# Half of a normalised input multiplied between modulation slabs, thirteen places for late slabs, and the last recurrent gates moved behind a gate tile

## The reference: one decoder layer, cut to what matters

```python
mod = silu(c) @ w_ada + b_ada            # (9, 6144): six blocks of 1024
sh1, sc1, g1, sh2, sc2, g2 = split(mod, 6)
h = rmsnorm(x, norm_pre_mix) * (1 + sc1) + sh1
q, k, v, g, xr, gr = split(h @ w_in)     # xr, gr: 1536 wide, 12 tiles of 128
...                                      # retention over q, k, v, gated by g
xc = causal_conv(xr)                     # 4 taps
r = sigmoid(xc @ w_rg_a + b_rg_a); i = sigmoid(xc @ w_rg_x + b_rg_x)   # block diagonal, 12 blocks
a = exp(-8 * r * softplus(-lru_param))
hseq = scan(a, sqrt(1 - a * a) * i * xc) # the recurrence over time
rnn_y = hseq * gelu(gr)
ga, gb = sigmoid(h @ w_mgate + b_mgate)  # 8 tiles each
mixed = (ga * (ret_y @ w_br_ret) + gb * (rnn_y @ w_br_rnn)) @ w_out
x = x + g1 * rmsnorm(mixed, norm_post_mix)
h2 = rmsnorm(x, norm_pre_ffn) * (1 + sc2) + sh2
x = x + g2 * rmsnorm((silu(fg) * fu) @ w_ffn_out, norm_post_ffn)       # fg, fu = split(h2 @ w_ffn_in)
```

## Time and profile before

| | |
|---|---|
| median of three runs | 1472.25 us (1471.32 to 1474.86) |
| the profiled execution's own time | 1477.67 us |
| its span | 1475.9 us |
| granted clock of PE, mean over the span | 0.974 |
| PE busy | 95% of the span |
| DVE, ACT, POOL busy | 51%, 35%, 12% |
| data moved | 172.71 MB, mean 117 GB/s |

### The profile page before, as it was taken

How to read it: one execution, slowest core, us unless ns; L and a number is a source line. 1 busy time by engine, 2 the same in 40 slices (tenths; PEclk the granted TensorE clock), 3 DMA queues, 4 the chain that set the end, 5 groups by cost and what they waited for, 6 DMA issues and landing times.

```text
span 1475.9 us, 24107 instructions
## 1 busy us (share of the span) xinstructions
PE 1397.5 (95%) x10324; PEld 1301.5 (88%) x10324; DVE 759.6 (51%) x1042; ACT 515.5 (35%) x715; POOL 183.1 (12%) x284
## 2 busy tenths in 40 slices
PE   5799999899999999999999999999889999999995
PEld 2799998777897798799879888999789999999995
DVE  3459888412245476348536753875843333332225
ACT  4376778111233331333234233335422222222221
POOL 1022231000013213302220330000000000000000
PEclk8799999999899899999999999999999999999998
DMA  8312222466524325423441443235012222222331
GB/s 334 114 58 86 72 73 71 143 228 241 189 72 157 122 94 176 156 84 115 162 152 65 157 158 115 83 102 206 1 57 86 87 87 86 87 85 78 90 92 61
DMA packets 49931, 172.71 MB, mean 117 GB/s; under 512 B 5536, under 2 KB 7712, under 8 KB 49568
## 3 DMA queue, kind: packets, MB, share of 16 engines
q1 hardware_dynamic: 39456, 135.51, 27.6%
q0 software_dynamic: 9216, 33.56, 6.6%
q10 hardware_dynamic: 1152, 2.10, 0.4%
HBM read 149.82 MB, written 21.32 MB: 116 GB/s over the span
## 4 chain that ended last, share of the span: by engine, by line
PE 64%; DVE 6%; issue 1%; DMA 1%; ACT 1%; SPq 0%; DVEq 0%
PE ps L746 51%; PE ps L755 3%; PE ps L969 2%; PE ps L980 2%; PE ps L952 1%; PE ps L996 1%; PE ps L1006 1%; PE ps L998 1%; DMA raw<-in_w_out 1%; DVE x_res L1851 1%; DVE rsn L1846 1%; DVE mo L1850 1%; DVE s_lo L1667 1%; PE ps L909 0%; PE ps L922 0%
## 5 line engine op out<-in xcount | busy, mean ns | idle before, releaser
L746 PE MATMUL ps<-h_hi,w_hi 128*128 128x272 f32 x2096 | 445.4, 294 | 17.5 <-DVE w_lo L1484 10.3
L746 PE MATMUL ps<-h_hi,w_lo 128*128 128x272 f32 x2096 | 438.1, 291 | 0.0
L746 PE MATMUL ps<-h_lo,w_hi 128*128 128x272 f32 x2096 | 436.8, 290 | 0.0
L1484 DVE TENSOR_TENSOR w_lo<-raw,w_hi 128x1024 fp32r<-128x1024 f32 (+2 forms) x190 | 228.7, 1206 | 335.6 <-ACT w_hi L1146 332.5
L746 PEld LDWEIGHTS ps<-h_hi,w_hi 128*128 128x128 f32 x2096 | 336.2, 191 | 23.7 <-issue 8.9
L746 PEld LDWEIGHTS ps<-h_lo,w_hi 128*128 128x128 f32 x2096 | 334.1, 191 | 0.0
L746 PEld LDWEIGHTS ps<-h_hi,w_lo 128*128 128x128 f32 x2096 | 331.8, 191 | 0.0
L1146 ACT ACTIVATE w_hi<-raw 128x1024 fp32r<-128x1024 f32 (+2 forms) x190 | 195.4, 1029 | 306.3 <-PE ps L746 161.6
L1767 DVE SCALAR_TENSOR_TENSOR state<-state,ps 128x512 f32<-128x512 f32 x64 | 41.1, 683 | 113.5 <-PE ps L1006 113.4
L746 PE MATMUL ps<-a_hi,w_hi 128*128 128x272 f32 x308 | 64.4, 291 | 2.1 <-DVE a_lo L1493 2.1
L746 PE MATMUL ps<-a_lo,w_hi 128*128 128x272 f32 x308 | 64.4, 290 | 0.0
(11 more groups left out here) (242 smaller groups left out, 1953.0 us busy)
## 6 DMA issues: line engine op xcount, KB each, us to landing
raw<-in_w_head SPq DMA_DIRECT2D x48, 512.0 KB, 3.6
raw<-in_w_fin SPq DMA_DIRECT2D x38, 512.0 KB, 3.5
ada_late<-in_w_ada SPq DMA_DIRECT2D x32, 512.0 KB, 4.3
state<-in_state POOLq DMA_DIRECT2D x32, 512.0 KB, 4.1
out_rs<-state POOLq DMA_DIRECT2D x32, 512.0 KB, 3.4
raw<-in_w_rnn SPq DMA_DIRECT2D x24, 512.0 KB, 3.6
ada_raw<-in_w_ada SPq DMA_DIRECT2D x16, 512.0 KB, 14.8
raw<-in_w_bret SPq DMA_DIRECT2D x16, 512.0 KB, 3.5
```

Of the source, the lines that this page charges most:

```text
L746: mm = nc.tensor.matmul(dst[:, half, :], a, b[:, half * HALF:(half + 1) * HALF], start=first and j == 0, stop=last and j == 2)
L1484: V.tensor_tensor(lo[:, 0:cols], raw_slab(i)[0][:, 0:cols], hi[:, 0:cols].bitcast(F32), ALU.subtract).then_inc(lo_ready, 1)
```

## The change

Four edits.

1. **Start.** PE turns the row of block 0 right after block 0. Block 1 accumulates in bank 7 (after ACT has read the sums of squares there), and between its slabs PE multiplies the first half of `h`: after slabs 1 to 4 one k-step of `xr` 0 each, after slabs 5 and 6 two k-steps of `gr` 0 each. Then it turns the row of block 1, and multiplies the second half of `h` into both tiles. DVE makes `w_lo` of `xr` 0 before `first_input(0)`; ACT does the first splits only in the first of its two rounds.
2. **Late slabs.** `ADA_RING` is 13: three places as before, ten in the memory of the recurrences (`rec`), which may be filled once all of `y` and the outputs of the recurrences are made. The first three are loaded behind `rg_w`.
3. **SP's loop** issues, for part i, late slabs up to 2i + 12 (at most 32) and then the weight slab two beyond part i.
4. **Last gates.** PE's `recurrent_gates(11)` and ACT's `gates(11)` and `roots` come behind `gb` 4.

```diff
--- before.py
+++ after.py
@@ -71,7 +71,8 @@
 
 RAW = 2
 STATES = 3
-ADA_RING = 3
+ADA_RING = 13
+ADA_EARLY = 3
 RING = 3
 AHEAD = 2
 COLS = 1024
@@ -411,23 +412,26 @@
         gbr = sb(gbr_scope, "gbr", [P, KD, T])
         rnn = ExitStack()
         ada_row = sb(rnn, "ada_row", [P, ADA_COLS])
-        ada_late = sb(rnn, "ada_late", [P, ADA_RING, COLS])
+        ada_late = sb(rnn, "ada_late", [P, ADA_EARLY, COLS])
         rnn_out = sb(rnn, "rnn_out", [P, NR, 36])
         rg_w = sb(rnn, "rg_w", [P, NR, 2, P])
         y_hi = sb(rnn, "y_hi", [P, NR, T], F32R)
         y_lo = sb(rnn, "y_lo", [P, NR, T], F32R)
-        xp = sb(rnn, "xp", [P, 2, 3 + SEQ])
-        xs = sb(rnn, "xs", [P, 2, NB, 3 + TS])
-        xc = sb(rnn, "xc", [P, 2, T])
-        gelu = sb(rnn, "gelu", [P, 3, T])
-        rr = sb(rnn, "rr", [P, 2, T])
-        ii = sb(rnn, "ii", [P, 2, T])
-        uu = sb(rnn, "uu", [P, 2, T])
-        su = sb(rnn, "su", [P, 2, T])
-        ee = sb(rnn, "ee", [P, 2, T])
-        bb = sb(rnn, "bb", [P, T])
-        hs = sb(rnn, "hs", [P, T])
-        h0a = sb(rnn, "h0a", [P, NB])
+        rec = ExitStack()
+        xp = sb(rec, "xp", [P, 2, 3 + SEQ])
+        xs = sb(rec, "xs", [P, 2, NB, 3 + TS])
+        xc = sb(rec, "xc", [P, 2, T])
+        gelu = sb(rec, "gelu", [P, 3, T])
+        rr = sb(rec, "rr", [P, 2, T])
+        ii = sb(rec, "ii", [P, 2, T])
+        uu = sb(rec, "uu", [P, 2, T])
+        su = sb(rec, "su", [P, 2, T])
+        ee = sb(rec, "ee", [P, 2, T])
+        bb = sb(rec, "bb", [P, T])
+        hs = sb(rec, "hs", [P, T])
+        h0a = sb(rec, "h0a", [P, NB])
+        rec.close()
+        ada_more = sb(rnn, "ada_more", [P, ADA_RING - ADA_EARLY, COLS])
         rnn.close()
 
 
@@ -630,6 +634,11 @@
                 return early_raw0[:, n, :] if n < 4 else early_raw1[:, n - 4, :], early_in[n], 16, None
             return raw[:, n % RAW, :], raw_in[n % RAW], 16 * (n // RAW + 1), pl.kinds[kind][n - RAW] if n >= RAW else None
 
+        def late_slab(n):
+
+            i = n % ADA_RING
+            return ada_late[:, i, :] if i < ADA_EARLY else ada_more[:, i - ADA_EARLY, :]
+
         def scores(j):
 
             at = sum(SEQ - i * P for i in range(j))
@@ -668,9 +677,11 @@
 
                 while late[0] < n:
                     j = late[0]
+                    if j == ADA_EARLY:
+                        recurrences_done()
                     if j >= ADA_RING:
                         sp.wait_ge(late_used, j - ADA_RING + 1)
-                    sp.dma_start(ada_late[:, j % ADA_RING, :], w["w_ada"][FIRST_BLOCKS + j // KD, j % KD])\
+                    sp.dma_start(late_slab(j), w["w_ada"][FIRST_BLOCKS + j // KD, j % KD])\
                         .then_inc(late_in[j % ADA_RING], 16)
                     late[0] += 1
 
@@ -700,13 +711,18 @@
             sp.wait_ge(h_ready, KD)
             sp.wait_ge(c4_ready, 1)
             sp.dma_start(rg_w[:], w["w_rg"]).then_inc(rg_in, 16)
-            load_to(pl.slab[("bn", 0, "w", 0)])
+            def recurrences_done():
+
+                sp.wait_ge(last_saved, NR)
+                sp.wait_ge(tails_saved, NR)
+                sp.wait_ge(y_ready, NR)
+
+            load_late(ADA_EARLY)
+            load_to(pl.slab[("bn", 1, "w", 0)])
             for m in range(KD):
                 for part in range(2):
-                    load_to(pl.slab[("bn", m, "w", part)])
-                    load_late(4 * m + 2 * part + 2)
-            sp.wait_ge(last_saved, NR)
-            sp.wait_ge(tails_saved, NR)
+                    load_late(min(4 * m + 2 * part + ADA_RING, 4 * KD))
+                    load_to(pl.slab[("bn", m, "w", part)] + 2)
             sp.dma_start(out["rnn"], rnn_out[:]).then_inc(stored, 16)
             load_to(pl.slab[("v", 0, 1, "w", 0)])
             rnn_memory_free(sp)
@@ -755,7 +771,7 @@
                     mm = nc.tensor.matmul(dst, a, b[:, cols_of(half)], start=first and j == 0, stop=last and j == 2)
                 return mm
 
-            def project(key, parts, hi, lo, ready=None, base=0, after=None, before_last=None, before_tile=None):
+            def project(key, parts, hi, lo, ready=None, base=0, after=None, before_last=None):
 
 
                 claim(key)
@@ -764,8 +780,6 @@
                     s = pl.slab[(*key, "w", i)]
                     pe.wait_ge(lo_ready, s + 1)
                     for j in range(n):
-                        if before_tile is not None and k in before_tile:
-                            before_tile[k]()
                         if ready is not None:
                             pe.wait_ge(ready, base + k + 1)
                         mm = three_passes(out_tile(key), s, j * P, hi[:, k, :], lo[:, k, :],
@@ -837,12 +851,36 @@
                 pe.wait_ge(row_ready, b + 1)
                 ada_turn(ada_row0[:, b, :], ps[:, 4 + b, :], turned0)
 
-            for b in range(FIRST_BLOCKS):
-                for k in range(KD):
-                    pe.wait_ge(ada_in[b * KD + k], 16)
-                    modulation(2 + b, k, ada_raw[:, b * KD + k, :], block_done)
-                    if b and k == 2:
-                        turn_first(0)
+            def first_slab(b, k):
+                pe.wait_ge(ada_in[b * KD + k], 16)
+                modulation((2, 7)[b], k, ada_raw[:, b * KD + k, :], block_done)
+
+            def first_tiles(name, ks):
+
+                key = (name, 0)
+                s = pl.slab[(*key, "w", 0)]
+                if ks[0] == 0:
+                    claim(key)
+                    pe.wait_ge(lo_ready, s + 1)
+                for k in ks:
+                    pe.wait_ge(h_ready, k + 1)
+                    mm = three_passes(out_tile(key), s, k * P, h_hi[:, k, :], h_lo[:, k, :], k == 0, k == KD - 1)
+                if ks[-1] == KD - 1:
+                    mm.then_inc(multiplied, 1)
+
+            for k in range(KD):
+                first_slab(0, k)
+            turn_first(0)
+            pe.wait_ge(std_ready, 1)
+            for k in range(KD):
+                first_slab(1, k)
+                if 1 <= k <= 4:
+                    first_tiles("xr", (k - 1,))
+                if k in (5, 6):
+                    first_tiles("gr", (2 * k - 10, 2 * k - 9))
+            turn_first(1)
+            for name in ("xr", "gr"):
+                first_tiles(name, range(KD // 2, KD))
 
 
             def recurrent_gates(n):
@@ -862,15 +900,15 @@
                 ada_turn(ada_row, dst[:, 0, :], full)
 
             for n in range(NR):
-                project(("xr", n), [KD], h_hi, h_lo, h_ready if n == 0 else None, 0,
-                        before_tile=None if n else {KD // 2: lambda: turn_first(1)})
                 if n:
+                    project(("xr", n), [KD], h_hi, h_lo)
                     recurrent_gates(n - 1)
-                project(("gr", n), [KD], h_hi, h_lo)
-                if n == NR - 1:
-                    recurrent_gates(n)
+                if n:
+                    project(("gr", n), [KD], h_hi, h_lo)
                 for m in GATE_TILES.get(n, ()):
                     project(("gb", m), [KD], h_hi, h_lo)
+                    if n == NR - 1 and m == GATE_TILES[n][0]:
+                        recurrent_gates(n)
             for m in range(KD):
 
                 def modulate(part, m=m):
@@ -879,7 +917,7 @@
                         if k == 0:
                             take_pair(("ad", b))
                         pe.wait_ge(late_in[n % ADA_RING], 16 * (n // ADA_RING + 1))
-                        modulation(4, k, ada_late[:, n % ADA_RING, :], late_used)
+                        modulation(4, k, late_slab(n), late_used)
 
                 b = FIRST_BLOCKS + m // 2 - 1
                 project(("bn", m), BN_PARTS, y_hi, y_lo, y_ready if m == 0 else None, 0,
@@ -1191,8 +1229,9 @@
                wait=False)
             for b in range(FIRST_BLOCKS):
                 act.wait_ge(block_done, KD * (b + 1))
-                do(A(ada_row0[:, b, :], ps[:, 2 + b, 0:ADA_COLS], ACT.Copy), row_ready, wait=False)
-                split_to(pl.slab[("gr", 0, "w", 0)])
+                do(A(ada_row0[:, b, :], ps[:, (2, 7)[b], 0:ADA_COLS], ACT.Copy), row_ready, wait=False)
+                if b == 0:
+                    split_to(pl.slab[("gr", 0, "w", 0)])
                 hi_of_first(b)
 
 
@@ -1250,12 +1289,12 @@
                     act.wait_ge(y_ready, n - 2)
                 wait_tile(act, ("gr", n))
                 do(A(halves(gelu[:, n % 3, :]), out_tile(("gr", n)), ACT.Gelu_apprx_tanh), *took(("gr", n)), wait=False)
-                if n == NR - 1:
-                    gates(n)
-                    roots(roots_at(NR))
                 for m in GATE_TILES.get(n, ()):
                     ahead(("gb", m))
                     evacuate(("gb", m), gbr[:, m, :], ACT.Sigmoid, bias=vcol("b_gb", m))
+                    if n == NR - 1 and m == GATE_TILES[n][0]:
+                        gates(n)
+                        roots(roots_at(NR))
             for m in range(KD):
```

(1 more changed line is left out.)

## The result

The changed kernel took 1464.54 us (median of four runs, 1463.08 to 1465.7) against 1473.46 for the kernel before: a ratio of 0.994, 95% interval 0.9923 to 0.9958, that is 8.9 us less. A repetition on another occasion (experiment 9) gave 0.9955 (0.9939 to 0.9971), 6.4 us less. The forecast was 11.2 less, 1461.1 us.

A forecast was written before the change was run, and what follows sets the result against it. TensorE was taken as the bound, busy 1397.5 of 1475.9 us, so only its stalls and lower-clock stretches pay. Start +4.2, branch stage −15.7 and burst +0.3 gave −11.2 from 1472.25: 1461.1 us, range 1456.5 to 1468.

The forecast's parts named there:

- inner band: Whole kernel: the forecast case, a time within 1458.5 to 1463.5 us, given a chance of 0.60.
- rival 3: Branch stage: the burst of late slabs stalls the fourth part, its slab 2.0 us late; +3, 1464 us; chance 0.11.
- Start: Kernel start up to the second xr tile: first-half chain, late slabs in SP's queue and clock together cost +4.2 us.
- second `first_input`: Start, DVE's step for the second half: begins at 43.8 instead of 44.23, −0.4 us.
- Rival 1: Start: the lower clock lasts through the interleaved stretch, +6.1 instead of −0.4, 1467.6 us; chance 0.13.
- The late slabs' 3.9: Start, SP's queue: three late slabs issued ahead of the second xr slab delay its landing by 3.9 us.
- The clock term: Start: after PE's longer idle before the second xr tile, up to 1.5 us more at lower clock, +0.7 us.
- Last gates: Last recurrent gates moved behind a gate tile: costs and gains nothing, as DVE stays the bound there.
- the term of −10.3: Branch stage: slabs issued one part sooner remove all stalls but the burst's, 86.55 instead of 96.85 us.
- Burst: Branch stage: ten late slabs queued once y is complete delay the fourth part's slab, +0.3 us, bounds 0 to 3.
- Rival 4: Branch stage: queue far below full rate in the burst, under 238 GB/s; kernel slower, 1475 us at 220; chance 0.04.
- End of the stage: End of branch stage: wait before the last turn shrinks, −3.0 us; the turn and tiles behind run at full clock, −2.4.

The follow-up runs named there:

- experiment 9: The changed kernel run again with no edit, for a second profile; ratio 0.9955 (0.9939 to 0.9971) to the kernel before.
- experiment 1: Only the start edit made, late slabs and last gates as in the kernel before; ratio 0.9999 (0.9982 to 1.0015) to the kernel before.
- experiment 5: Changed kernel, but PE finishes block two's slabs and one xr k-step, turns the row, then multiplies the rest of h's first half; ratio 0.9916 to before, 1460.11 us.
- experiment 4: Changed kernel with the three early late slabs issued behind the second xr and gr slabs instead of ahead; ratio 0.9927 to the kernel before, median 1461.63 us.
- experiment 3: Changed kernel with the last recurrent gates back in their old place; ratio 0.994 (0.9923 to 0.9956) to the kernel before.
- experiment 6: Changed kernel with the burst of ten late slabs cut to five ahead of the fourth branch slab and four behind; ratio 0.9948 to the kernel before, 1464.44 us.
- experiment 12: Kernel of experiment 8, but last gates moved as in the change and DVE's last splits moved up; ratio 0.9784 to the kernel before, median 1441.11 us.
- experiment 11: The kernel before run again with no edit, for a second profile; ratio 1.0013 (0.9993 to 1.0032), span 1468.4 us.
- experiment 7: Changed kernel with the second xr and gr slabs loaded before SP waits for the whole of h; ratio 0.9882 to the kernel before, median 1453.64 us.
- experiment 8: Changed kernel with block two's slabs first, burst cut, second xr and gr slabs early, last gates in old place; ratio 0.9817 to the kernel before, 1445.06 us.

## Why the prediction came out as it did

The time, 8.9 us below before and 6.4 on repetition, lies inside the range (1456.5 to 1468) and on the forecast side, less far down than the 11.2 that were forecast. It is not in the inner band, 1458.5 to 1463.5, that was given 0.60: 1464.54 is where rival 3 had its 1464. Of the 3.4 us above the forecast, 1.2 are the median of the kernel before, 1473.46 with a fourth run where the prediction had 1472.25. Step by step:

**Start: forecast +4.2, measured 64.83 − 62.48 = +2.35 to PE's second xr tile, +2.5 to the gates behind it.** The second `first_input` at 43.77 looks as forecast (−0.46 against −0.4), but that is luck of this pair of profiles: over seven profiles against three it is +0.9 (experiment 1). The k-steps between the slabs are what it hangs on, for without them it comes at 37.20 (experiment 5). Rival 1 (lower clock throughout, near 50) did not happen. The late slabs' 3.9 measured 3.74 (experiment 4). The term that was missing is the landing of `rg_w`: 6.4 to 6.5 us in all eleven profiles with a new start, 7.4 to 7.5 in all three with the old one, so −1.0. The clock term (+0.7) was +0.2: the tile took 72.58 − 64.83 = 7.75 us from its first matmul to the gates, against 70.07 − 62.48 = 7.59. PE was low when it started again after 9.42 us (0.79 us for the pair of matmuls, 0.49 in the earlier trace rows); but it had gone low before the change too, 1.3 us after it started again from a wait of 2.87 us. The Trainium skill, TensorE: Matmul & The Clock Gate, What's actually happening, has the array throttled unless activity releases it; the first of these rows agrees. In the means of several profiles the start is worth more: the first recurrent gates come at 73.4 in the four profiles with both of the edits that meet there (the changed kernel, experiments 3, 6 and 9) and at 69.7 in the two of the kernel before, +3.8, near the forecast +4.2.

**Last gates: forecast 0, measured none** (experiment 3, to within its interval). The 5.9 us before gb6 are DVE's order, as argued: moving DVE's own splits removes them (experiment 12, which has the gates moved too), moving the gates alone doesn't.

**Branch stage: the term of −10.3 was mis-sized.** The mechanism was right: with 13 places every wait for a branch slab but one went, and the unstalled period held (5.71 to 5.73 us between parts, 5.94 to 5.95 with a turn). Two sizes were off. First, the 96.85 us that the term was taken from belong to one long execution; two other profiles of the same code have 93.34 and 94.06 (experiments 1 and 11). The changed kernel's sixteen parts spread over 88.7 us (372.55 − 283.89) and, repeated, 87.9; without the burst's wait of 2.10 the first is 86.6, as forecast. That is −8.2 against the long profile, −5.4 between the means of the other two and of these two, and −6.5 with all three in the mean. The prediction went through the profiled execution's time, 5.4 us above the median, and took the whole stall from it; the part of a stall that only this execution had is not there to be won in the median. Second, the burst.

**Burst: forecast +0.3, measured 2.10 and 1.48 (rival 3's wait of 2.0, without the fall of the clock that it added: PE ran at 1.00 behind it).** SP's queue and ACT's timeline of the changed kernel, and windows (length, clock, DMA share, GB/s):

```profile
274.39 5.80 SPq L684 DMA_DIRECT2D ada_more<-in_w_ada  x10
284.60 0.81 SPq L684 DMA_DIRECT2D ada_late<-in_w_ada  x2
285.44 0.43 SPq L696 DMA_DIRECT2D raw<-in_w_brnn  x1
```

```profile
296.61 0.84 ACT L1184 ACTIVATE w_hi<-raw 128x768 fp32r<-128x768 f32 x1 [15.67 <-DMA raw<-in_w_brnn]
```

```profile
276.00:278.00 2.00, 1.00 1.03 245
278.00:280.00 2.00, 1.00 0.83 297
280.00:282.00 2.00, 1.00 1.03 416
...
294.00:296.00 2.00, 1.00 1.02 405
```

The slab issued at 285.44 was split at 296.61. The forecast had it landed at 291.1 (0.9 before 292.0), which with everything shifted by 2.55 us is 293.6. The full rate was as assumed, 401 to 422 GB/s from 280 to 296, but the first six microseconds ran at 245 to 297 (192 to 330 in experiment 6, with five late slabs in place of ten), and transfers issued after this slab, from 290.30 on, were in flight with it. The same section of the Trainium skill (DMA: Bandwidth & Descriptors, Queues, rings and completion order) says that a later transfer may finish before an earlier one; this row fits that, and no run here shows which one did. That the order of the burst makes the wait is shown: with five late slabs ahead instead of ten it went (experiment 6). That edit does two things, though. In the changed kernel SP stands before this slab until PE has used the first late slab (283.89) and so issues it only at 285.44; in experiment 6 nothing holds it and it is issued at 278.51. Which of the two counts was not told apart; that the DMA share is 1.01 to 1.05 from 280 to 296 speaks for the bytes ahead of it. Rival 4 (under 238 GB/s) did not happen.

**End of the stage: forecast −3.0 and −2.4.** The wait fell from 3.47 to 0.51, and the turn and two tiles behind it from 14.87 to 374.56 + 12.02 − 374.12 = 12.46 (12.46 again in the repetition): −3.0 and −2.4, as forecast from that profile. Its size, too, was partly of that execution: in experiments 1 and 11, with the same stage, the wait was 3.25 and 3.35, and the turn and two tiles took 393.34 − 379.34 = 14.00 and 392.99 − 379.01 = 13.98. Against these the terms are −2.8 and −1.5.

**The sum.** In the two profiles PE had the two head tiles behind it 11.03 us sooner (386.58 against 397.61), nearly the forecast −11.2, by two errors that cancel: 1.7 us too much at the start, and 1.8 too little for the burst. The medians moved less, and over several profiles the terms do too:

| term | forecast | the two profiles | means of several |
|---|---|---|---|
| start | +4.2 | +2.5 | +3.8 |
| sixteen parts, with the burst | −10.0 | −8.2 | −6.5 |
| wait before the last turn | −3.0 | −3.0 | −2.9 |
| turn and two tiles | −2.4 | −2.4 | −1.8 |
| sum | −11.2 | −11.1 | −7.4 |

The last column has the start from two profiles before and four after, as above, and the rest from three of the old stage (before, experiments 1 and 11) and two of the new (changed, experiment 9). It lies between the measured −8.9 and −6.4. Which of the three old profiles is typical stays open: without the long one the column gives −5.9. Of the remaining 1.6 us between the two spans, 1.4 lie in the stretch of experiment 9: from PE's wait for the state split to the turn after it (line 922 before, 960 after) 514.81 − 494.32 = 20.49 us before and 502.52 − 483.39 = 19.13 after.

**Where more was to be had.** The chain at the start ran through the k-steps between the slabs (experiment 5) and through a load that was issued after h and did not need h (experiment 7). Experiments 5, 7 and 8 took some 4, 11 and 19 us more than the change out of the same places.

## What to carry to other kernels

Size a stall from more than one profile of the kernel before: small waits with a fall of the clock behind them differ by some us between executions, and a gain worked out from a long one is too large for the median. One pair of profiles can also make a term look right that is not, as the second `first_input` here. When a load is moved in a queue, ask what small load stands behind it and who waits for that one, and which loads wait for a condition that they don't need. When one engine is freed to arrive earlier, ask what is released by something that did not move: in experiment 12 the burst, in the change the second row.

## What was not expected of the hardware

- `rg_w` (1536 KB, same issue order, nothing ahead of it) took 7.4 to 7.5 us to land in the three profiles with the old start and 6.4 to 6.5 in all eleven with a new one. The cause is open.
- The clock fell to 0.50 behind a wait of 2.35 us in the first head in some executions of one kernel and not in others, and behind a wait of 1.81 us in one profile of the kernel before, while 2.10 us (changed kernel, before the fourth part) did not bring it down.
- The queue moved 245 to 297 GB/s for the first six us in which its ten 512 KB loads were being issued, and only then 401 to 422.
